# A macaron encoder block: a feed-forward chunk sent and turned later, activation sums made earlier, SiLU's table loaded ahead

## The reference

```
def swiglu(x, w_in, w_out):
    gate, up = jnp.split(x @ w_in, 2, axis=-1)
    return (jax.nn.silu(gate) * up) @ w_out

h = h + 0.5 * swiglu(rmsnorm(h, ffn1_norm), ffn1_w_in, ffn1_w_out)   # 2048 -> 2 x 5632 -> 2048
...  (a mixing stage, a cross attention)
h = h + 0.5 * swiglu(rmsnorm(h, ffn2_norm), ffn2_w_in, ffn2_w_out)
```

## Time and profile before

| | |
|---|---|
| three runs | 2129.96, 2130.85, 2134.89 us; median 2130.85 |
| the profiled execution | 2129.56 us, span 2127.5 us |
| TensorE busy | 2106.6 us, 99% |
| VectorE, ScalarE busy | 1534.0 us (72%), 1089.3 us (51%) |
| DMA | 472.37 MB, 222 GB/s in the mean |

### The profile page before, as it was taken

How to read it: one execution, slowest core, us unless ns; L and a number is a source line. 1 busy time by engine, 2 the same in 40 slices (tenths; PEclk the granted TensorE clock), 3 DMA queues, 4 the chain that set the end, 5 groups by cost and what they waited for, 6 DMA issues and landing times.

```text
span 2127.5 us, 27271 instructions
## 1 busy us (share of the span) xinstructions
PE 2106.6 (99%) x9405; PEld 1740.4 (82%) x9405; DVE 1534.0 (72%) x1647; ACT 1089.3 (51%) x1249; POOL 38.4 (2%) x50
## 2 busy tenths in 40 slices
PE   9999999999999999999999999999999999999998
PEld 7788888888888888888888888887887888888887
DVE  7999999984555576566565656569999999964444
ACT  6555555553444455456544545455555555543433
POOL 0000000000000031000000000000000000000000
PEclk9999999999999999999999999999999999999999
DMA  7676667776666676765587766575667767775554
GB/s 278 223 231 218 221 231 228 226 245 239 208 228 214 220 265 218 237 213 184 178 285 239 237 208 191 189 247 198 229 226 223 224 217 221 225 287 195 190 188 157
DMA packets 185317, 472.37 MB, mean 222 GB/s; under 512 B 17056, under 2 KB 67616, under 8 KB 185120
## 3 DMA queue, kind: packets, MB, share of 16 engines
q1 hardware_dynamic: 183088, 464.11, 66.1%
q0 software_dynamic: 1728, 6.82, 0.9%
q10 hardware_dynamic: 432, 0.53, 0.1%
HBM read 443.60 MB, written 27.79 MB: 222 GB/s over the span
## 4 chain that ended last, share of the span: by engine, by line
PE 60%; DVE 18%; DMA 11%; issue 8%; ACT 2%; DVEq 0%; SPq 0%; ACTq 0%; POOLq 0%; POOL 0%
PE acc L1869 18%; PE acc L1871 18%; PE acc L1872 18%; DMA raw<-in_ffn_w_in 11%; DVE w_lo L1186 9%; DVE t_raw L1312 2%; DVE raw L1310 2%; DVE t_raw L1309 2%; DVE stage L1293 1%; PE acc L1893 1%; PE acc L1892 1%; PE acc L1894 1%; DVE stage L1226 1%; ACT w_hi L727 1%; DVE shared L1348 0%
## 5 line engine op out<-in xcount | busy, mean ns | idle before, releaser
L1186 DVE TENSOR_TENSOR w_lo<-raw,w_hi 128x1024 fp32r<-128x1024 f32 x765 | 924.8, 1223 | 477.1 <-ACT w_hi L727 474.9
L727 ACT ACTIVATE w_hi<-raw 128x1024 fp32r<-128x1024 f32 x765 | 796.8, 1056 | 857.5 <-PE acc L1872 532.7
L1869 PE MATMUL acc<-w_hi,a_hi 128*128 128x512 f32 x744 | 290.3, 390 | 0.5 <-DVE w_lo L1186 0.5
L1872 PE MATMUL acc<-w_hi,a_lo 128*128 128x512 f32 x744 | 289.6, 389 | 0.0
L1871 PE MATMUL acc<-w_lo,a_hi 128*128 128x512 f32 x744 | 289.5, 389 | 0.0
L1869 PE MATMUL acc<-w_hi,b_hi 128*128 128x512 f32 x576 | 225.6, 392 | 0.0
L1871 PE MATMUL acc<-w_lo,b_hi 128*128 128x512 f32 x576 | 224.3, 389 | 0.0
L1872 PE MATMUL acc<-w_hi,b_lo 128*128 128x512 f32 x576 | 224.2, 389 | 0.0
L1892 PE MATMUL acc<-w_hi,a_hi 128*128 128x512 f32 x460 | 179.0, 389 | 0.0
L1893 PE MATMUL acc<-w_lo,a_hi 128*128 128x512 f32 x460 | 179.0, 389 | 0.0
L1892 PE MATMUL acc<-w_hi,b_hi 128*128 128x512 f32 x460 | 179.0, 389 | 0.0
(11 more groups left out here) (273 smaller groups left out, 2645.1 us busy)
## 6 DMA issues: line engine op xcount, KB each, us to landing
raw<-in_ffn_w_in SPq DMA_DIRECT2D x349, 512.0 KB, 4.2
raw<-in_ffn_w_out SPq DMA_DIRECT2D x176, 512.0 KB, 4.3
raw<-in_w_mix_in SPq DMA_DIRECT2D x80, 512.0 KB, 4.4
raw<-in_w_ckv SPq DMA_DIRECT2D x64, 512.0 KB, 4.3
memq<-bounce SPq DMA_DIRECT2D x196, 128.0 KB, 4.3
bounce<-stage SPq DMA_DIRECT2D x37, 512.0 KB, 3.1
raw<-in_w_mix_out SPq DMA_DIRECT2D x32, 512.0 KB, 4.5
raw<-in_w_cq SPq DMA_DIRECT2D x32, 512.0 KB, 4.3
```

The lines of the kernel that those rows point to most:

```text
L727: eng.activation(w_hi[:, u % RING], raw[:, u % RING], ACT.Copy).then_inc(w_hi_done, 1)
L1186: eng.tensor_tensor(w_lo[:, u % RING], raw[:, u % RING], w_hi[:, u % RING].bitcast(f32), ALU.subtract).then_inc(w_lo_done, 1)
L1869: eng.matmul(dst, x_hi[:, rows], w_hi[:, slot, i], start=start and i == 0, stop=False)
L1872: last = eng.matmul(dst, x_lo[:, rows], w_hi[:, slot, i], start=False, stop=stop and i == UK - 1)
```

## The change

Three parts, all in `ffn_in` and the first pairs before it.

1. In a pass, `hidden` moves from behind unit 3 to behind unit 7; the send from before load 7 to before load 12; the fetch from before load 10 to before load 14; the turn from behind the third `t_lo_part` to behind unit 12's `w_lo`; `fill_hi` from behind unit 10 to behind `copy_p1`; `fill_lo` to behind the first of the adds for the gate (L1348).
2. The activation sums stand at units 5, 7 and 9 of FFN1's first pair and 9, 11 and 13 of FFN2's, in place of 10, 12 and 14. The clearing of `shared` goes from unit 8 to unit 4.
3. In either first pair ScalarE runs a SiLU on one column, which loads SiLU's table, at unit 14 (FFN1) or 6 (FFN2).

```diff
-SEND_AT = 7
-MIX_AT = [10, 12, 14][-FAST:]
-FETCH_AT = 10
+SEND_AT = 12
+FETCH_AT = 14
+X_MIX_AT = [5, 7, 9]
+H3_MIX_AT = [9, 11, 13]
...
@@ ScalarE, pair(j, hid_dst)
                         split(base, j, FAST_AT[s] + 2, PAIR)
-                        if s == FAST - 1:
-                            fill_hi(turned, number(TURNS, hid) + j, hid_dst, src=stage4)
                         split(base, j, FAST_AT[s] + 3, PAIR)
...
                     eng.activation(copy_p1, sum_p1, ACT.Copy).then_inc(p1_copied, 1)
+                    fill_hi(turned, number(TURNS, hid) + j, hid_dst, src=stage4)
                     split(base, j, PAIR - 3, PAIR)
...
@@ ScalarE, first_pair_of_x (in first_pair_of_h3: p == 6, H3_MIX_AT)
-                    if p - 1 in MIX_AT:
-                        s = MIX_AT.index(p - 1)
+                    if p == 14:
+                        eng.activation(first_exp[:], ones[:, 0:1], ACT.Silu)
+                    if p - 1 in X_MIX_AT:
+                        s = X_MIX_AT.index(p - 1)
...
@@ VectorE, pair(j, hi, lo)
                         fast_lo(j, s)
-                        if s == FAST - 1:
-                            turn(number(TURNS, hid) - 1 + j, stage4)
                         unit_lo(j, FAST_AT[s] + 2)
                         if s == 0:
                             up_drained(j - 1)
-                        if s == FAST - 1:
-                            fill_lo(split_number(hid) - 1 + j, lo, hi, src=stage4)
                         unit_lo(j, FAST_AT[s] + 3)
-                        if s == 0:
+                        if s == 1:
                             hidden(j - 1)
                     for p in range(4 * FAST, PAIR - 3):
                         unit_lo(j, p)
+                    turn(number(TURNS, hid) - 1 + j, stage4)
 
                     eng.wait_ge(p1_copied, done)
                     eng.tensor_tensor(shared[:, 0], sum_p6, copy_p1, ALU.add).then_inc(p6_added, 1)
+                    fill_lo(split_number(hid) - 1 + j, lo, hi, src=stage4)
                     unit_lo(j, PAIR - 3)
...
                     eng.wait_ge(w_used, base + PAIR * j + GATE_END)
+
+                    eng.wait_ge(t_read, number(FILLS, hid) + j)
                     eng.tensor_tensor(stage[:, 0], acc[:, 0], copy_p1, ALU.add)
...
@@ VectorE, first_pair_of_x (the same in first_pair_of_h3 with H3_MIX_AT)
-                    if p - 2 in MIX_AT:
-                        mix_parts_lo(FFN1_IN, MIX_AT.index(p - 2), a_hi, a_lo)
-                    if p in MIX_AT:
-                        mix_parts(MIX_AT.index(p), a_hi, a_lo)
-                    if p == 8:
+                    if p - 2 in X_MIX_AT:
+                        mix_parts_lo(FFN1_IN, X_MIX_AT.index(p - 2), a_hi, a_lo)
+                    if p in X_MIX_AT:
+                        mix_parts(X_MIX_AT.index(p), a_hi, a_lo)
+                    if p == 4:
                         chain(eng.memset(shared[:], 0.0))
```

More of the change, by code:

```diff
@@ L1136, in first_pair_of_h3 @@
                         turned_h3_hi(DC - 1)
-                    if p - 1 in MIX_AT:
-                        s = MIX_AT.index(p - 1)
+                    if p == 6:
+                        eng.activation(first_exp[:], ones[:, 0:1], ACT.Silu)
+                    if p - 1 in H3_MIX_AT:
+                        s = H3_MIX_AT.index(p - 1)
                         mix_parts_hi(FFN2_IN, s, b_hi, HEAD_PAIR.index((1, s)) + 1)
@@ L1366, in ffn_in @@
                 eng.sem_inc(gate_read, 1)
-                mixed = (a_hi, a_lo) if base == FFN1_IN else (b_hi, b_lo)
-                mix_parts_lo(base, MIX_AT.index(PAIR - 2), *mixed)
                 with eng.Fori(1, DC + 1) as j:
@@ L1802, in first_pair_of_h3 @@
                                 GAIN_AT["ffn2_norm"] + 12)
[L1803 to L1807, removed]
+                    if p - 2 in H3_MIX_AT:
+                        mix_parts_lo(FFN2_IN, H3_MIX_AT.index(p - 2), b_hi, b_lo)
+                    if p in H3_MIX_AT:
+                        mix_parts(H3_MIX_AT.index(p), b_hi, b_lo)
+                    if p == 4:
                         chain(eng.memset(shared[:], 0.0))
```

## The result

| | before | after |
|---|---|---|
| median, same chip | 2132.87 us (4 runs, 2129.96 to 2136.16) | 2148.94 us (4 runs, 2148.05 to 2157.06) |
| ratio | 1 | 1.0083, 95% interval 1.0053 to 1.0113 |
| profiled execution, span | 2129.56, 2127.5 | 2157.06, 2155.0 |

The change makes the kernel slower, by 16 us between the medians and by 27.5 us between the two profiled spans. The profiled execution of after is the highest of its four; the others lie within 1.1 us of each other. So the stages are compared in the profiled pair, and the size of the whole is taken from the ratio.

What follows compares the result with a forecast made beforehand. TensorE, busy 2106.6 of 2127.5 us, was taken as the bound; after the change VectorE would pace the loop. Loops +33.9, ahead of FFN1 -5.4, FFN2 -4.8: +23.7 on 2129.56, or 2153.3, stated as 2154; range 2122 to 2174.

Steps and rivals of the forecast that it cites:

- The hole: VectorE's 2.53 us idle before the third group's sums in each loop pass; claimed gone once `hidden` moves there.
- Rival D: Hole before the third group stays in part, unit 9's load being slow itself: +1.2 us a pass, 2175; chance 0.08.
- The block of turn, copy and `fill_lo`: Behind unit 12 in each loop pass: from turn to the end of `fill_lo` takes 3.76 us as one block.
- The fetch: Issued behind load 13; last piece lands 6.0 us after issue, in place at T + 6.7, so the turn waits.
- T: End of a loop pass's third `t_lo_part` on VectorE, the reference moment for the forecast's times.
- W: VectorE's wait for the fetch at the turn: 3.4 us in every pass, ends 1.9 and 4.8.
- The pass: VectorE's chain per loop pass: 40.63 + 3.4 = 44.0 us, above TensorE's 41.48, adding 33.9 us over eighteen.
- Ahead of FFN1: Before the loops: first T 5.4 us earlier in FFN1, at 73.2, and 4.8 us earlier in FFN2, at 1475.6.
- TensorE's waits: Waits on `t_lo_part` in the loops should move from third to first group and grow to 30 to 50 us.
- Rival E: TensorE's waits of 2.5 us a loop pass bring its clock down: at most 30 us, 2184; chance 0.05.
- Rival B: Fetch lands as when alone, 4.2 us: about 2121, or 2110 without a wait; turning point 4.7 us; chance 0.14.
- C: Rival in between: fetch lands at 4.5 to 4.9 us, gain and loss cancel, 2130; chance 0.08.

Runs made afterwards that it cites:

- e3: The kernel before with one number changed: the fetch is issued behind load 10, not load 9; 2116.62 us, ratio 0.9910.
- e1: The kernel before with only parts 2 and 3 of the change (earlier activation sums, early SiLU table load), loop unchanged; 2130.35 us, ratio 0.9972.
- e7: The changed kernel with the fetch issued one load sooner, behind load 12 and not 13; 2111.14 us, ratio 0.9903.
- e8: The changed kernel with the fetch behind load 12 and the send before load 11, each one load sooner; 2108.75 us, ratio 0.9892.
- e2: The kernel before with only part 1 of the change (the loop moves), first pairs unchanged; 2160.79 us, ratio 1.0108.
- e10: The changed kernel with only the send one load sooner, before load 11 and not 12; 2153.34 us, ratio 1.0089.

## Why the prediction was right, step by step

1. **The hole.** Forecast gone, and gone. Rival D falls. That the fetch behind load 9 made most of it is shown by e3.
2. **The block of turn, copy and `fill_lo`.** Forecast 3.76 us; 1677.86 - 1674.10 = 3.76. The 0.80 that VectorE waits for `hid_hi` is the copy left bare.
3. **The fetch.** Forecast: last issue at T + 0.75, 6.0 us to landing, in place at T + 6.7, W = 3.4. Measured: T + 0.83, 6.11, T + 6.94, W = 3.5. The mean of before's landings held, and so did its ends: the waits run from 2.0 to 4.4 us where 1.9 and 4.8 were named. The reason given, that the surroundings are alike, holds as far as loads go: in both, two loads are still to land when the fetch starts. The moment of issue was partly luck. The forecast took it from load 13 and left the send out. The send took 5.4 us and not 3.0, and in 12 of the 20 passes it was its landing that let the fetch go; it came within 0.4 us of load 13's own time.
4. **The pass.** Forecast 44.0; measured 44.1 in FFN1 and 44.1 in FFN2.
5. **Ahead of FFN1.** Forecast -5.4 with T at 73.2; measured -6.5, T at 72.1. The stop at the first `t_lo_part` is 0.61 us and not 1.4. In FFN2 forecast -4.8, measured -2.9, counted from FFN1's last T. Alone, in e1, this part gives 6 us by the ratio, with the reserve made there.
6. **TensorE's waits.** Forecast on `t_lo_part` at the first group, 30 to 50 us in all. They stand there, but with 20.9 us, and another 10 us are on the `w_lo` just ahead; 31 in sum. That is less than the 47 us which 18 passes of 2.6 us lose. In part a bracket understates a stop. At this one of 1.14 us the starts are 1.52 and 0.34 us apart where 0.23 is usual, 1.40 us lost (two rows before, one behind):

```profile
1601.30 0.40 PE L1895 MATMUL tp<-w_lo,mix_hi 128*128 128x512 f32 x1
1601.54 0.39 PE L1896 MATMUL tp<-w_hi,mix_lo 128*128 128x512 f32 x1
1603.06 0.50 PE L1894 MATMUL aux<-t_hi_part,mix_hi 128*128 128x512 f32 x1 [1.14 <-DVE t_lo_part L1330]
1603.40 0.40 PE L1895 MATMUL aux<-t_lo_part,mix_hi 128*128 128x512 f32 x1
```

7. **The rivals.** **Rival E** (clock) falls: with stops of up to 1.2 us, two in a pass, the granted clock falls nowhere before the last 5 us of the span. **Rivals B** and **C** fall for after, but B's arithmetic did not. It set the turning point at a landing of 4.7 us and the time without a wait at 2110. e7 lands at 3.6 and takes 2111; e8 takes 2109.

**The size of the sum.** Forecast +23.7 us on the profiled execution; the profiled pair shows +27.5, the medians +16, the ratio +18. So the mechanism is right, and the size lies between the two. The terms are off by -1.1, +1.2, +1.9 and +1.3 us, in the order in which they come, with 0.6 behind the loops. The other three runs of after lie 8 us below the profiled one. How the wait differs in them no profile shows; with 20 waits on a landing, 0.4 us in each would do it. And the median of before is 2 us higher than the one forecast from, as a fourth time, 2136.16, has joined the three. What stays open is which of the times is the usual one: e2 spread over 9 us and e10 over 5, e3 and e8, in which next to nothing waits for the fetch, over 1.4 and 0.8 us; the kernel before, with its hole, over 6.

What I did not see, though it stood in the rows, is how near the other side was. Rival B asked for a fetch that lands as if alone. I looked for that in chance (one in 20 passes). It hung on load 13 being issued in front of the fetch or behind it, which is the one difference between after and e7.

## What to carry to other kernels

When a step that waits for a transfer is moved, measure the distance from the issue of that transfer to the moment at which its reader is ready, before and after. Here, from the fetch's first piece to the turn, it shrank from 11.9 us to 4.2, and where a hole of 2 us a pass was filled there came a wait of 3.5. Where the DMA engines are busy for two thirds of the time, as here, ask what is issued just in front of the transfer that is wanted first, and try a prefetch that has time in hand behind it: that one number was worth 38 us here. And before a hole is filled with other work, look at what causes it; moving the cause by one place gave 19 us with nothing else touched.

## What the runs showed of the hardware

- Among transfers that SP issues, one place in the order counts. With load 13 (512 KB) issued 0.7 us ahead of a fetch of 4 x 128 KB (after) the last piece lands 6.11 us after its issue; with load 13 issued 0.6 us behind that piece (e7) it lands after 3.60. The Trainium skill (DMA: Bandwidth & Descriptors, Queues, rings and completion order) says that all DMAs that SP issues share one ring on each of the 16 DMA engines, which are consumed in ring order; e7 against after agrees.
- The order is not the whole of it. In e8 a load 0.56 us ahead of the fetch goes with a landing of 4.12 us. And a load is held up by what is issued behind it: load 9 lands after 5.7 us with the fetch 0.6 us behind it (before) and after 4.4 with load 10 some 2.8 us behind it (e3). The second is not what service strictly in the order of issue would give.
- The same send of 512 KB to device memory takes 5.4 us in the mean of the passes in after and e7, where load 11 goes out 1.4 us ahead of it, and 3.7 and 3.4 us in e10 and e8, where load 11 goes out 0.7 us behind it. The send starts at T - 6.4 in all four, so this is the place of one load again.
- A stop of 2.44 us ahead of FFN1's loop went with a granted clock of 0.86 over 12 us; the 39 stops of up to 1.2 us in after's loops went with no fall of it.
